# Weight sums by accumulating DMAs, token sums on VectorE, bias rows and decays on ScalarE: one change to a trunk of attention layers and feed-forward blocks

## The chip, the core and the metric

The kernel runs on one core of a Trainium2 chip. The metric is the device time of one execution, in microseconds (us); the median of several runs is given. The engines are TensorE (PE, matmuls; PEld is its weight load), VectorE (DVE), ScalarE (ACT), GpSimd (POOL) and SyncE (SP, which here only issues DMAs). Each engine works through its own list in order and stops at a wait until a semaphore has reached a value. Transfers issued by SP and by GpSimd run in two queues (q1 and q0) on the same 16 DMA engines.

## The reference, cut to what matters

```python
x = x + 0.5 * swiglu(rms_norm(x, g), w_in, w_out)    # FFN, four times
def swiglu(h, w_in, w_out):
    a, b = jnp.split(h @ w_in, 2, axis=-1)           # w_in: 1024 x 5632, w_out: 2816 x 1024
    return (jax.nn.silu(a) * b) @ w_out
# FFN0, sparse attention (NSA), FFN1, shared keys and values, FFN2, forgetting attention (FoX), FFN3
# FoX: softmax(q k^T * scale + c[query] - c[key], causal) v,   c = cumsum(log_sigmoid(f))
# NSA: scores get a bias by bucket of the distance, one column of rel_bias per head
```

There are 256 tokens of 1024 values, in float32.

## The kernel before, in words

**Products.** Each float32 operand is split into a high part (rounded to the matmul's type) and a low part (the rest). A product is three matmuls: high by high, high by low, low by high (`three`, L571 to L573).

**Units.** All weights pass through TensorE in units of 128x2048 values (1.05 MB). For unit u ScalarE casts the high part (`hi(u)`, L1154, `whi`), VectorE subtracts to get the low part (`lo(u)`, L1586, `wlo`), and TensorE multiplies. `whi` and `wlo` are rings of three, so `hi(u)` waits until TensorE is done with unit u-3. Plain units are loaded by SP into a ring of three `raw` buffers (`load`, L448); a load waits until the low part of the buffer's last unit is done. SP works through all of its loads and waits in one order.

**An FFN.** Its hidden columns lie in 11 chunks of 256. The order of the 39 units is `a0 b0 a1 b1 o0 a2 b2 o1 | M1 M5 o2 M2 M6 M3 M7 M4 | a5 b5 o3 a6 b6 o4 | M1 M5 o5 M2 M6 o6 M3 M7 M4 | a9 b9 o7 a10 b10 o8 o9 o10`. `a` and `b` are the two halves of a chunk's input weights (24 matmuls each), `o` its output rows. Chunks 3 and 4, and 7 and 8, are done as pairs: a 2x2 block product with seven products (M1 to M7, 12 matmuls each) in place of eight. For them the four weight blocks B11, B12, B22, B21 of 1.05 MB are loaded by SP (`pair_weights`, L477) into `nat`, `nat`, `work` and `xn`, one after each of four ring loads, from `o0` on for the first pair and from `b5` on for the second. VectorE makes four sums: T1 = B12-B11 (L1674, into `kT` or `low`), T3 = B22-B12 in place (L1681), T2 (L1687) and T4 (L1694). M1, M2, M3 use plain blocks, M5, M7, M6, M4 the sums. The second pair's first load waits for the first pair's sums and for the low part of its M7.

**Token sums.** The pairs need sums of token blocks too. GpSimd joins the high and low parts of the tokens (L2187, twice), multiplies them by the norm's factors (L2193, twice) and makes four sums (L2198 to L2204); ScalarE and VectorE split them (L1231, L1666) before the first pair.

**Hidden.** After a chunk's `b`, ScalarE makes silu(a) (L1215), VectorE multiplies by b (L1644, `gg`), TensorE transposes the result after the `o` units that stand between (L706, into `tb`), ScalarE and VectorE split it (L1221, L1651). In the list of ScalarE for chunk 5 the cast of `a6` stands ahead of silu, that of `b6` behind it; the same holds in the other chunks for the unit three after `a` and the one after that.

**GpSimd's other work.** In FFN0 it builds NSA's bias rows with 32 small copies (L2223), stores them (L2230) and loads them back per head (L2235). In the stage of the shared keys it loads FoX's c for all heads (L2262), and near the end of FFN2 it adds masks and c by query to them, 16 instructions (L2273 to L2277).

Of the kernel before, what the change touches and what calls it, by code (L numbers as in the profile page):

```python
# [27 lines left out]
P = 128  # L28
# [22 lines left out]
RING = 3  # L51
KINDS = "nnnsnnsnn"
# [74 lines left out]
def ring_loads():  # L127

    count, last, loads = [0] * RING, [None] * RING, {}
    for u in range(U_END):  # L130
        if not any(b <= u < b + FFN_UNITS and ORDER[u - b][0] not in "abo" for b in U_FFN):
# [39 lines left out]
def yoco_trunk(nc, x, norm_g, ffn_w_in, ffn_w_out, nsa_w_in, nsa_cmp_pos, nsa_cmp_w1, nsa_cmp_w2,  # L171
               nsa_w_out, rel_bias, kv_norm_g, fox_w_kvf, fox_b_f, fox_w_q, fox_w_out, final_g, out):
    ctx = ExitStack()
    with ctx:
# [87 lines left out]
        b11, b12, b21, b22 = nat[:, 0:UNIT], nat[:, UNIT:2 * UNIT], xn[:, :, :].rearrange("p t n -> p (t n)"), work[:, 0:UNIT]  # L262
# [24 lines left out]
        def combined(f):  # L287

            return low[:, :] if f == 2 else kT[:, :, :].rearrange("p k n -> p (k n)")

# [12 lines left out]
        def unit_source(u):  # L303

            if u in LOADS:
                return raw[LOADS[u][0]][:, :]
            f, b, (kind, j) = of_ffn(u)
            x = combined(f)
            return {"M1": b11, "M2": b21, "M3": b22, "M5": x, "M6": b11, "M7": b12, "M4": x}[kind]
# [31 lines left out]
        s_rows = sem("bias_rows")  # L341
        s_rows_out = sem("bias_rows_stored")
# [10 lines left out]
        s_b11 = sem("b11_loaded")  # L353
        s_b12 = sem("b12_loaded")
# [73 lines left out]
        s_cq = sem("c_by_query")  # L428
        s_decay = sem("decay_ready")
# [17 lines left out]
        def _(sp):  # L447
# [29 lines left out]
            def pair_weights(f, n, i):  # L477
# [21 lines left out]
            def ffn(f):  # L499
                b, n, i = U_FFN[f], 0, None  # L500
                for u, (kind, j) in enumerate(ORDER, b):
# [12 lines left out]
                    if i is not None and kind in "abo":  # L514
# [624 lines left out]
        def _(act):  # L1139
            def hi(u):  # L1140
# [5 lines left out]
                elif kind in ("M1", "M2", "M3"):  # L1146
                    arrived = {"M1": s_b11, "M2": s_b21, "M3": s_b22}[kind]
                    act.wait_ge(arrived, 32 * (len(PAIRS) * f + PAIRS.index(j) + 1))
                else:
                    done = ["M5", "M7", "M6", "M4"].index(kind) + 1  # L1150
                    act.wait_ge(s_tw, 4 * (len(PAIRS) * f + PAIRS.index(j)) + done)
# [81 lines left out]
            def ffn_chunk(f, j, rows):  # L1233
# [13 lines left out]
                hi(a + 3)  # L1247
                act.wait_ge(s_g, 2 * (NSEG * f + i))
# [4 lines left out]
                for r in rows:  # L1253
                    u = b + UNIT_OF["o", r]
                    chunk_hidden_hi(f, j)
                    if u + 3 < b + FFN_UNITS:
                        hi(u + 3)

# [313 lines left out]
        def _(dve):  # L1572
# [95 lines left out]
            def t1_weights(f, j):  # L1668

                n = len(PAIRS) * f + PAIRS.index(j) + 1  # L1670
                dve.wait_ge(s_b11, 32 * n)
                dve.wait_ge(s_b12, 32 * n)
                dve.wait_ge(s_alo, 4 * f + 4)
                dve.tensor_tensor(combined(f), b12, b11, ALU.subtract).then_inc(s_tw, 1)  # L1674

            def t3_weights(f, j):

                n = len(PAIRS) * f + PAIRS.index(j) + 1
                dve.wait_ge(s_b22, 32 * n)
                dve.wait_ge(s_tw, 4 * n - 3)  # L1680
                dve.tensor_tensor(b12, b22, b12, ALU.subtract).then_inc(s_tw, 1)  # L1681

            def t2_weights(f, j):

                n = len(PAIRS) * f + PAIRS.index(j) + 1
                dve.wait_ge(s_tw, 4 * n - 2)
                dve.tensor_tensor(b11, b12, b11, ALU.add).then_inc(s_tw, 1)  # L1687

            def t4_weights(f, j):
# [3 lines left out]
                dve.wait_ge(s_tw, 4 * n - 1)  # L1693
                dve.tensor_tensor(combined(f), b21, b11, ALU.subtract).then_inc(s_tw, 1)  # L1694

            def ffn_chunk(f, j, rows):
# [12 lines left out]
                if pair:  # L1709
                    t1_weights(f, pair)  # L1710
# [4 lines left out]
                if pair:  # L1715
                    t3_weights(f, pair)
# [9 lines left out]
            def ffn_pair(f, j, rows):  # L1726
# [4 lines left out]
                lo(m["M1"] + 3)  # L1731
                t4_weights(f, j)
                lo(m["M5"] + 3)
# [11 lines left out]
                dve.tensor_tensor(c12, tb[1][:, :], c12, ALU.add).then_inc(s_c12, 1)  # L1745
# [8 lines left out]
                dve.tensor_tensor(c22, c22, u3, ALU.add).then_inc(s_c22, 1)  # L1754
# [359 lines left out]
            dve.wait_ge(s_decay, H // 4)  # L2114
# [34 lines left out]
        def _(pool):  # L2149
# [29 lines left out]
            def token_sums(f):  # L2179
# [9 lines left out]
                pool.wait_ge(s_whole, 2 * f + 2)  # L2189
                pool.wait_ge(s_rc, f + 1)  # L2190
                for t in range(NT):
                    tok = slice(t * P, (t + 1) * P)
                    pool.tensor_tensor(m[:, :, tok], m[:, :, tok],  # L2193
                                       rstd_row[:, tok].unsqueeze(1).broadcast_to([P, KT, P]),
                                       ALU.mult).then_inc(s_an, 1)
                pool.wait_ge(s_an, 2 * f + 2)
                a11, a12, a21, a22 = [quarter(m, a) for a in ("A11", "A12", "A21", "A22")]
                pool.tensor_tensor(four(c22), a21, a22, ALU.add).then_inc(s_as, 1)  # L2198
                pool.wait_ge(s_as, 4 * f + 1)
                pool.tensor_tensor(a21, a11, a21, ALU.subtract).then_inc(s_as, 1)  # L2200
                pool.wait_ge(s_as, 4 * f + 2)
                pool.tensor_tensor(a11, four(c22), a11, ALU.subtract).then_inc(s_as, 1)
                pool.wait_ge(s_as, 4 * f + 3)
                pool.tensor_tensor(a12, a12, a11, ALU.subtract).then_inc(s_as, 1)  # L2204

            token_sums(0)
# [6 lines left out]
            pool.wait_ge(s_used, 8)  # L2213
# [3 lines left out]
            after = UNIT_OF["a", PAIRS[0] + 2]  # L2217
            pool.wait_ge(s_setup, 2)
            pool.wait_ge(s_used, after + 1)
            starts = bucket_starts()  # L2220
            for b in range(NB):
                near, far = starts[b], starts[b + 1] - 1
                pool.tensor_copy(rows[:, SEQ - 1 - far:SEQ - near],  # L2223
                                 tbT[:, b:b + 1].broadcast_to([H, far - near + 1]))
            pool.memset(rows[:, SEQ:2 * SEQ], NEG).then_inc(s_rows, 1)
            pool.wait_ge(s_rows, 1)

            pool.dma_start(scratch_b.rearrange("c h m -> h c m"),  # L2230
                           rows.unsqueeze(1).broadcast_to([H, 16, 512])).then_inc(s_rows_out, 16)
            pool.wait_ge(s_rows_out, 16)
            for h in range(H):
                pool.wait_ge(s_used, after + 4 + h)
# [23 lines left out]
            token_sums(1)  # L2258
# [6 lines left out]

            pool.wait_ge(s_cb, 16)
            pool.wait_ge(s_cq, 1)
            token_sums(2)
# [33 lines left out]
```

## Time and profile before

| | |
|---|---|
| time, median of 3 runs | 1044.06 us (1043.92 to 1044.14) |
| profiled execution | 1042.84 us, its span 1041.1 us |
| TensorE busy | 1028.7 us (99%), granted clock 0.997 |
| VectorE, ScalarE, GpSimd busy | 765.6, 587.4, 151.6 us |
| DMA | 182.78 MB, mean 176 GB/s |

A profile shows one execution. In rows of the trace the first numbers are the start and the length in us; "x2" means that two instructions follow one another; brackets at the end give the idle time of the engine before the instruction and what ended it. The busy share of an engine tells how full it is over the whole span; whether a unit came late is seen from TensorE's waits.

### The profile page before, as it was taken

The page shows a single profiled execution, that of the slowest core. Times are in us where ns is not written, and L with a number is a line of the kernel's source. Part 1 is how long each engine was busy: PE and PEld are TensorE (multiplying, and loading weights), DVE is VectorE, ACT ScalarE, POOL GpSimd, SP SyncE. Part 2 cuts the span into 40 slices and gives each one's busy share as a digit, 9 for nine tenths or more (in the row PEclk, how much of TensorE's full clock was granted, in tenths as well). Part 3 has the DMA queues.
Part 4 walks back from the last instruction along what each step waited for, and adds up shares of the span by engine and source line. Part 5 has one row for each costly group of instructions (what it writes and reads, how often), then busy time and mean ns, then how long its engine had stood idle before and what let it go on. Part 6 is the DMA issues. An engine that isn't in the chain of part 4 may idle for free.

```text
span 1041.1 us, 13003 instructions
## 1 busy us (share of the span) xinstructions
PE 1028.7 (99%) x5076; PEld 847.2 (81%) x5076; DVE 765.6 (74%) x925; ACT 587.4 (56%) x732; POOL 151.6 (15%) x140
## 2 busy tenths in 40 slices
PE   8999999999999999999999999999999999999997
PEld 7888888888888888788888888788888888878886
DVE  6897875677576579868656769868766657986864
ACT  6565454656476565555456555546446656555543
POOL 3613111000013150000000150000470015000000
PEclk9999999999999999999999999999999999999999
DMA  9919456457401492742746692752646149274261
GB/s 307 340 23 375 151 155 224 144 181 216 148 2 41 123 341 61 273 171 82 228 145 194 220 345 83 252 193 81 206 158 202 42 141 341 64 269 175 82 202 41
DMA packets 112349, 182.78 MB, mean 176 GB/s; under 512 B 5960, under 2 KB 67504, under 8 KB 112160
## 3 DMA queue, kind: packets, MB, share of 16 engines
q1 hardware_dynamic: 110656, 176.18, 50.2%
q0 software_dynamic: 1456, 5.72, 1.9%
q8 instruction: 40, 0.66, 0.3%
q14 instruction: 21, 0.17, 0.0%
q10 hardware_dynamic: 176, 0.05, 0.0%
HBM read 180.34 MB, written 1.59 MB: 175 GB/s over the span
## 4 chain that ended last, share of the span: by engine, by line
PE 92%; DVE 4%; issue 2%; ACT 1%; DMA 0%; ACTq 0%; DVEq 0%
PE acc L571 13%; PE acc L573 13%; PE acc L572 13%; PE inb L571 12%; PE inb L573 12%; PE inb L572 12%; PE acc L837 2%; PE inb L864 2%; PE tb L849 2%; PE tb L572 1%; PE tb L573 1%; PE tb L571 1%; PE tb L706 1%; DVE wlo L1586 1%; PE inb L861 1%
## 5 line engine op out<-in xcount | busy, mean ns | idle before, releaser
L1586 DVE TENSOR_TENSOR wlo<-raw,whi 128x2048 fp32r<-128x2048 f32 x131 | 319.8, 2443 | 107.9 <-ACT whi L1154 107.7
L1154 ACT CAST whi<-raw 128x2048 fp32r<-128x2048 f32 x131 | 250.5, 1915 | 52.3 <-PE inb L573 19.9
L571 PE MATMUL inb<-whi,thi 128*128 128x512 f32 x528 | 210.1, 398 | 0.6 <-DVE work L1751 0.6
L573 PE MATMUL inb<-whi,tlo 128*128 128x512 f32 x528 | 206.2, 391 | 0.0
L572 PE MATMUL inb<-wlo,thi 128*128 128x512 f32 x528 | 205.9, 390 | 0.0
L571 PE MATMUL acc<-whi,fhi 128*128 128x512 f32 (+1 forms) x384 | 149.0, 388 | 0.0
L573 PE MATMUL acc<-whi,flo 128*128 128x512 f32 (+1 forms) x384 | 148.3, 386 | 0.0
L572 PE MATMUL acc<-wlo,fhi 128*128 128x512 f32 (+1 forms) x384 | 148.2, 386 | 0.0
L571 PEld LDWEIGHTS inb<-whi,thi 128*128 128x128 f32 x528 | 99.3, 188 | 21.4 <-issue 2.2
L573 PEld LDWEIGHTS inb<-whi,tlo 128*128 128x128 f32 x528 | 99.2, 188 | 21.2
L572 PEld LDWEIGHTS inb<-wlo,thi 128*128 128x128 f32 x528 | 99.4, 188 | 19.4
L571 PE MATMUL acc<-whi,thi 128*128 128x512 f32 x224 | 89.5, 399 | 0.8 <-DVE tlo L1614 0.6
L573 PE MATMUL acc<-whi,tlo 128*128 128x512 f32 x224 | 87.6, 391 | 0.0
L572 PE MATMUL acc<-wlo,thi 128*128 128x512 f32 x224 | 87.4, 390 | 0.0
L573 PEld LDWEIGHTS acc<-whi,flo 128*128 128x128 f32 (+1 forms) x384 | 70.5, 184 | 15.9
L572 PEld LDWEIGHTS acc<-wlo,fhi 128*128 128x128 f32 (+1 forms) x384 | 70.5, 184 | 15.4
L571 PEld LDWEIGHTS acc<-whi,fhi 128*128 128x128 f32 (+1 forms) x384 | 70.5, 184 | 15.3
L1215 ACT ACTIVATE sa<-inb,rstd 128x256 f32<-128x256 f32 x48 | 20.2, 470 | 75.6 <-PE inb L573 75.6
L1221 ACT CAST fhi<-tb 128x512 fp32r<-128x512 f32 x28 | 16.4, 587 | 81.6 <-PE tb L706 81.6
L1154 ACT CAST whi<-nat 128x2048 fp32r<-128x2048 f32 x24 | 45.9, 1914 | 22.5 <-PE inb L573 15.4
L1586 DVE TENSOR_TENSOR wlo<-nat,whi 128x2048 fp32r<-128x2048 f32 x24 | 54.9, 2287 | 3.0 <-ACT whi L1154 2.8
L571 PEld LDWEIGHTS acc<-whi,thi 128*128 128x128 f32 x224 | 42.1, 188 | 10.8 <-DVE tlo L1614 1.0
(293 smaller groups left out, 1534.3 us busy)
## 6 DMA issues: line engine op xcount, KB each, us to landing
raw<-in_ffn_w_in SPq DMA_DIRECT2D x110, 512.0 KB, 5.2
raw<-in_ffn_w_out SPq DMA_DIRECT2D x88, 512.0 KB, 5.4
nat<-in_ffn_w_in SPq DMA_DIRECT2D x32, 512.0 KB, 6.4
raw<-in_nsa_w_in SPq DMA_DIRECT2D x20, 512.0 KB, 4.2
work<-in_ffn_w_in SPq DMA_DIRECT2D x16, 512.0 KB, 8.2
xn<-in_ffn_w_in SPq DMA_DIRECT2D x16, 512.0 KB, 10.4
raw<-in_fox_w_kvf SPq DMA_DIRECT2D x16, 512.0 KB, 4.3
raw<-in_nsa_cmp_w SPq DMA_DIRECT2D x8, 512.0 KB, 5.0
```

The costliest lines, as they stand in the source:

```text
L571: pe.matmul(o, lh, rh, start=start, stop=False, skip_group_check=True)
L572: pe.matmul(o, lh, rl, start=False, stop=False, skip_group_check=True)
L573: return pe.matmul(o, ll, rh, start=False, stop=stop, skip_group_check=True)
L706: mm = pe.transpose(tb[0][:, k * SEQ + t * P:k * SEQ + (t + 1) * P], gg[:, t, k * P:(k + 1) * P], ident[:, :])
L837: mm = pe.matmul(acc[2 * (n % 2) + h][:, c0:c0 + keys], qT[rows, p, t * P:(t + 1) * P], kT[rows, kidx, 0:keys], start=True, stop=True)
L849: mm = pe.transpose(tb[h][:, i * P:(i + 1) * P], probs[:, n % 2, c:c + P], ident[:, :])
L861: mm = pe.matmul(o0, pT[:, n % 2, h, 0:P], v(0), start=True, stop=True)
L864: mm = pe.matmul(o1, pT[:, n % 2, h, (1 + k) * P:(2 + k) * P], v(k), start=k == 0, stop=k == 1)
L1154: act.copy(whi[u % RING][:, :], unit_source(u)).then_inc(s_hi, 1)
L1215: act.activation(sa[:, t, :], banks[t][:, 0:FC], ACT.Silu, scale=rstd[:, t:t + 1]).then_inc(s_silu, 1)
L1221: act.copy(hidden_hi[:, k:k + 2, :].rearrange("p k n -> p (k n)"), tb[0][:, :]).then_inc(s_ghi, 1)
L1586: dve.tensor_tensor(wlo[u % RING][:, :], unit_source(u), whi[u % RING][:, :].bitcast(F32), ALU.subtract).then_inc(s_lo, 1)
```

## The change

- B11 is loaded twice: raw through the ring, where M1 is a plain unit now (`PLAIN`), and into `sum_a`. B22 is loaded twice too, into `sum_b` and into `work`. B12 is not loaded alone.
- GpSimd issues two accumulating DMAs per pair (`add_blocks`): `sum_a` += B12 when `sum_a` has landed, `sum_b` += B12 when `sum_b` has. These are T1 and T3, with other signs, and ScalarE casts them when the DMAs have landed.
- VectorE keeps two sums per pair, `sum_a` += B22 (T2) and `sum_a` += B21 (T4); T4 stands behind the low part of M6 instead of M2's. Two later adds become subtractions.
- The second pair's first load waits for the low part of M4 in place of M7.
- The token multiplies and sums move from GpSimd to VectorE, into chunk 1 behind the split of chunk 0's hidden values; GpSimd keeps the join.
- NSA's bias rows are copied by ScalarE in chunks 1 and 2 of FFN0, and their store and the small loads move accordingly; the loads per head wait for later units.
- FoX's masks are added by two accumulating DMAs (into `bias` and into `decay0`, which is loaded by itself), and c by query by ScalarE in chunks 1, 2, 5 and 9 of FFN2.

```diff
+PLAIN = ("a", "b", "o", "M1")
...
                 elif i == 0:
-                    u = b + UNIT_OF["M7", PAIRS[n - 1]]
-                    sp.wait_ge(s_tw, 4 * (len(PAIRS) * f + n))
+                    u = b + UNIT_OF["M4", PAIRS[n - 1]]
+                    sp.wait_ge(s_tw, 2 * (len(PAIRS) * f + n))
                     sp.wait_ge(s_lo, u + 1)
                 if i == 0:
-                    pair_in(f, j, 0, 0, b11, s_b11)
+                    pair_in(f, j, 0, 0, sum_a, s_la)
                 elif i == 1:
-                    pair_in(f, j, 0, 1, b12, s_b12)
+                    pair_in(f, j, 1, 1, sum_b, s_lb)
...
+                    elif kind == "M1":
+                        r = raw[LOADS[u][0]][:, :].rearrange("p (k n) -> p k n", k=4)
+                        w = ffn_w_in[f // 2, f % 2][0:512, j * FC:j * FC + CW].rearrange("(k p) n -> p k n", p=P)
+                        load(u, [(r[:, k:k + 2], w[:, k:k + 2]) for k in (0, 2)])
...
+                    n = len(PAIRS) * f + PAIRS.index(j) + 1
+                    ready = {"M2": (s_b21, 32 * n), "M3": (s_b22, 32 * n), "M5": (s_t1, 16 * n), "M7": (s_t3, 16 * n),
+                             "M6": (s_tw, 2 * n - 1), "M4": (s_tw, 2 * n)}
+                    act.wait_ge(*ready[kind])
...
+            def decays(j, i):
+
+                where = {1: 1, 2: 1, PAIRS[0] + 2: 0, PAIRS[1] + 2: 0}
...
+                act.wait_ge(s_mask1 if t else s_mask0, 16)
+                for h in range(4 * half, 4 * half + 4):
+                    d = bias[:, h, :] if t else decay0[:, h, :]
+                    ins = act.activation(d, d, ACT.Identity, bias=cq[:, t, h:h + 1])
+                ins.then_inc(s_decay, 1)
...
-            def t1_weights(f, j):
...
-                dve.tensor_tensor(combined(f), b12, b11, ALU.subtract).then_inc(s_tw, 1)
...
-            def t3_weights(f, j):
+            def token_sums(f):
...
+                m = whole_tokens(f)
+                dve.wait_ge(s_whole, 2 * f + 2)
+                dve.wait_ge(s_rc, f + 1)
...
                 elif before == 0:
                     chunk_hidden_lo(f, 0)
+                    token_sums(f)
...
                 lo(m["M1"] + 3)
+                lo(m["M5"] + 3)
                 t4_weights(f, j)
-                lo(m["M5"] + 3)
                 lo(m["M5"] + 4)
...
+            def add_blocks(f, n):
+
+                j, m = PAIRS[n], len(PAIRS) * f + n + 1
+                w = ffn_w_in[f // 2, f % 2][0:512, j * FC + DFF:j * FC + DFF + CW].rearrange("(k p) n -> p k n", p=P)
+                for to, begun, added in ((sum_a, s_la, s_t1), (sum_b, s_lb, s_t3)):
+                    pool.wait_ge(begun, 32 * m)
+                    pool.dma_start(to.rearrange("p (k n) -> p k n", k=4), w, accum_op=ALU.add).then_inc(added, 16)
```

## Rows read from the trace of the kernel before

**Rows 1.** The page: busy time of each engine.

```profile
PE 1028.7 (99%) x5076; PEld 847.2 (81%) x5076; DVE 765.6 (74%) x925; ACT 587.4 (56%) x732; POOL 151.6 (15%) x140
```

**Rows 2.** TensorE's waits: line, waited for, us in total, times, longest.

```profile
PE acc L917 <- POOL ident L2160: 1.6, 1, 1.6
...
PE inb L571 <- DVE work L1751: 0.6, 4, 0.2
```

**Rows 3.** Groups by line, VectorE: busy us, mean ns, idle before.

```profile
L1681 DVE TENSOR_TENSOR nat<-work,nat 128x2048 f32<-128x2048 f32 x8 | 18.3, 2283 | 0.0
```

**Rows 4.** Groups by line, GpSimd, then VectorE.

```profile
L2193 POOL TENSOR_TENSOR kT<-kT,work 128x1024 f32<-128x1024 f32 x6 | 21.9, 3667 | 25.4 <-ACT work L1243 25.4
...
L1754 DVE TENSOR_TENSOR work<-work 128x512 f32<-128x512 f32 x8 | 5.5, 692 | 0.3
...
L2140 DVE TENSOR_TENSOR xn<-xs,vx 128x1024 f32<-128x1024 f32 x2 | 2.5, 1225 | 0.1
```

**Rows 5.** Stretches: busy us of each engine, clock, DMA share, GB/s.

```profile
425.00:452.00 27.00, 26.84 (x124) 21.66 (x123) 20.30 (x18) 12.58 (x11) 0.00 (x0) 1.00 1.02 372
...
25.00:50.00 25.00, 25.00 (x117) 20.65 (x117) 19.85 (x18) 14.22 (x16) 17.17 (x6) 1.00 1.00 352
```

**Rows 6.** In order of time, VectorE (M7's and M4's low parts), then SP.

```profile
419.74 2.29 DVE L1586 TENSOR_TENSOR wlo<-nat,whi 128x2048 fp32r<-128x2048 f32 x1 [0.62 <-ACT whi L1154]
...
422.55 2.28 DVE L1586 TENSOR_TENSOR wlo<-kT,whi 128x2048 fp32r<-128x2048 f32 x1
...
422.11 0.88 SPq L475 DMA_DIRECT2D nat<-in_ffn_w_in  x2
```

**Rows 7.** In order of time: FFN1's second pair, ScalarE and VectorE; then FFN3's.

```profile
442.32 1.91 ACT L1154 CAST whi<-raw 128x2048 fp32r<-128x2048 f32 x1 [0.58 <-DMA raw<-in_ffn_w_in]
...
452.41 1.92 ACT L1154 CAST whi<-nat 128x2048 fp32r<-128x2048 f32 x1 [2.92 <-PE inb L573]
...
458.58 1.91 ACT L1154 CAST whi<-kT 128x2048 fp32r<-128x2048 f32 x1
...
444.26 2.29 DVE L1586 TENSOR_TENSOR wlo<-raw,whi 128x2048 fp32r<-128x2048 f32 x1 [1.91 <-ACT whi L1154]
...
939.26 2.29 DVE L1586 TENSOR_TENSOR wlo<-raw,whi 128x2048 fp32r<-128x2048 f32 x1 [2.15 <-ACT whi L1154]
...
947.16 1.91 ACT L1154 CAST whi<-nat 128x2048 fp32r<-128x2048 f32 x1 [2.67 <-PE inb L573]
```

**Rows 8.** FFN1 before its first pair: ScalarE, VectorE, SP, landings from 372 us.

```profile
386.45 0.59 ACT L1221 CAST fhi<-tb 128x512 fp32r<-128x512 f32 x1 [3.35 <-PE tb L706]
386.93 1.92 ACT L1154 CAST whi<-raw 128x2048 fp32r<-128x2048 f32 x1
...
397.42 0.84 ACT L1215 ACTIVATE sa<-inb,rstd 128x256 f32<-128x256 f32 x2 [3.53 <-PE inb L573]
...
377.17 2.88 DVE L1586 TENSOR_TENSOR wlo<-raw,whi 128x2048 fp32r<-128x2048 f32 x1 [1.18 <-ACT whi L1154]
...
376.27 1.25 SPq L475 DMA_DIRECT2D xn<-in_ffn_w_in  x2
...
xn<-in_ffn_w_in SPq DMA_DIRECT2D x2, 512.0 KB, 10.4
```

**Rows 9.** DMA at 585:597 us (two), 349:361, 98:107 (two), whole (one).

```profile
q0 software_dynamic: 144, 2.10, 45.0%
...
raw<-in_ffn_w_in SPq DMA_DIRECT2D x2, 512.0 KB, 9.5
...
raw<-in_ffn_w_in SPq DMA_DIRECT2D x2, 512.0 KB, 4.3
...
q0 software_dynamic: 144, 0.52, 29.8%
...
bias_rows_dram<-low POOLq DMA_DIRECT2D x1, 512.0 KB, 7.8
...
bias<-bias_rows_dram POOLq DMA_DIRECT2D x16, 128.0 KB, 3.2
```

More of the change, by code:

```diff
@@ L130, in ring_loads @@
     for u in range(U_END):
-        if not any(b <= u < b + FFN_UNITS and ORDER[u - b][0] not in "abo" for b in U_FFN):
+        if not any(b <= u < b + FFN_UNITS and ORDER[u - b][0] not in PLAIN for b in U_FFN):
             slot = len(loads) % RING
@@ L307, in unit_source @@
             f, b, (kind, j) = of_ffn(u)
-            x = combined(f)
-            return {"M1": b11, "M2": b21, "M3": b22, "M5": x, "M6": b11, "M7": b12, "M4": x}[kind]
+            return {"M2": b21, "M3": b22, "M5": sum_a, "M6": sum_a, "M7": sum_b, "M4": sum_a}[kind]
         onat = xn[:, :, :].rearrange("p t (h d) -> p t h d", h=H)
@@ L341, in yoco_trunk @@
         s_rows = sem("bias_rows")
+        s_fill = sem("bias_rows_filled")
         s_rows_out = sem("bias_rows_stored")
@@ L1247, in ffn_chunk @@
                 hi(a + 3)
+                if f == 2:
+                    decays(j, 0)
+                elif f == 0:
+                    bias_rows(j, 0)
                 act.wait_ge(s_g, 2 * (NSEG * f + i))
@@ L1257, in ffn_chunk, with bias_rows @@
                         hi(u + 3)
+                if f == 2:
+                    decays(j, 1)
+                elif f == 0:
+                    bias_rows(j, 1)
+            def bias_rows(j, i):
+                if j not in (1, 2):
+                    return
+                act.wait_ge(s_setup, 2)
+                starts = bucket_starts()
+                half = 2 * (j - 1) + i
+                for b in range(NB // 4 * half, NB // 4 * (half + 1)):
+                    near, far = starts[b], starts[b + 1] - 1
+                    ins = act.copy(rows[:, SEQ - 1 - far:SEQ - near], tbT[:, b:b + 1].broadcast_to([H, far - near + 1]))
+                ins.then_inc(s_rows, 1)
+            def decays(j, i):
+                where = {1: 1, 2: 1, PAIRS[0] + 2: 0, PAIRS[1] + 2: 0}
+                if j not in where:
+                    return
+                t, half = where[j], 2 * (j in (2, PAIRS[1] + 2)) + i
+                act.wait_ge(s_cq, 1)
+                act.wait_ge(s_mask1 if t else s_mask0, 16)
[3 more added lines that the diff above has]
+                ins.then_inc(s_decay, 1)
             def ffn_pair(f, j, rows):
@@ L1692, in t4_weights @@
                 dve.wait_ge(s_b21, 32 * n)
-                dve.wait_ge(s_tw, 4 * n - 1)
-                dve.tensor_tensor(combined(f), b21, b11, ALU.subtract).then_inc(s_tw, 1)
+                dve.tensor_tensor(sum_a, sum_a, b21, ALU.add).then_inc(s_tw, 1)
             def ffn_chunk(f, j, rows):
@@ L2188, in token_sums @@
                                        ALU.add).then_inc(s_whole, 1)
[L2189 to L2206, printed above, removed]
+            def add_blocks(f, n):
[4 more added lines that the diff above has]
+                    pool.dma_start(to.rearrange("p (k n) -> p k n", k=4), w, accum_op=ALU.add).then_inc(added, 16)
+            pool.memset(rows[:, SEQ:2 * SEQ], NEG).then_inc(s_fill, 1)
+            join_tokens(0)
+            add_blocks(0, 0)
+            pool.wait_ge(s_rows, 4)
+            pool.wait_ge(s_fill, 1)
+            pool.dma_start(scratch_b.rearrange("c h m -> h c m"),
+                           rows.unsqueeze(1).broadcast_to([H, 16, 512])).then_inc(s_rows_out, 16)
             small = [(gate_w[:, :, :], nsa_w_in[0, :, D + 6 * KVD:].rearrange("(k p) n -> p k n", p=P)),
@@ L2212, in _ @@
                      (bf[:, :], fox_b_f.rearrange("(h a) -> h a", a=1))]
-            pool.wait_ge(s_used, 8)
             for dst, src in small:
                 pool.dma_start(dst, src).then_inc(s_small2, 16)
[L2217 to L2231, printed above, removed]
+            for n in range(1, len(PAIRS)):
+                add_blocks(0, n)
             pool.wait_ge(s_rows_out, 16)
             for h in range(H):
-                pool.wait_ge(s_used, after + 4 + h)
+                pool.wait_ge(s_used, min(UNIT_OF["M4", PAIRS[-1]] + 1 + h // 2, FFN_UNITS))
                 pool.dma_start(bias[:, h, :], bass.AP(tensor=scratch_b.tensor, offset=h * 512 + P - 1,
@@ L2257, in _ @@
             pool.memset(vx[:, :].rearrange("p (i n) -> p i n", n=VP)[:, :, DH], 1.0).then_inc(s_ones, 1)
-            token_sums(1)
+            join_tokens(1)
+            for n in range(len(PAIRS)):
+                add_blocks(1, n)
             pool.wait_ge(s_neg, 1)
```

84 lines of the change are left out of this document (43 added, 41 removed).

## The prediction, made before the result was known

> **What bounds the kernel now.** I read the table of engines first: TensorE is busy 1028.7 us of a span of 1041.1 [rows 1]. The list of TensorE's waits comes next: its largest entry is 1.6 us, once, at the start, and the largest that belongs to the weight pairs is 0.6 us in four pieces, the wait for VectorE's add of `u3` [rows 2]. So TensorE goes from one weight unit to the next without a gap. The change removes no matmul. Whatever it frees on VectorE, GpSimd or ScalarE is worth nothing unless a TensorE wait ends earlier, and it costs nothing until a unit arrives late. The question is therefore how much room each unit has, and the smallest room is where it must be asked: in the stretches in which the DMA engines are full. The table of stretches shows one, behind the first load of FFN1's second pair: 372 GB/s and a DMA share of 1.02 from 425 to 452 us [rows 5]. A share of 1.02 is no spare at all. At 372 GB/s one block of 1.05 MB takes 2.8 us.
>
> **Part by part.**
>
> *Two weight sums fewer on VectorE.* Per pair T1 and T3 go, operations of one shape, 2.28 us each [rows 3]: 16 x 2.28 = 36.5 us of VectorE. TensorE hardly waits for it, so the gain is bounded by [rows 2], 0.6 us. I take 0: that wait (`u3` after the low part of `a5`) hangs on the cast of `a5`, not on a sum. T2 and T4 stay, T4 one unit later, still before its user.
>
> *Token sums to VectorE.* The two GpSimd multiplies took 3.67 us each [rows 4]. They become VectorE's, with the four sums. VectorE does a 128x1024 operation in 1.23 us and a 128x512 one in 0.69 [rows 4], so two and four make 2 x 1.23 + 4 x 0.69 = 5.2 us, once per FFN, right after the hidden split of chunk 0. Behind them wait the low part of `a2` and the gated tiles of chunk 1. In FFN1 VectorE was free from 377.17 - 1.18 = 376.0, and the low part of `a2` ran 377.2 to 380.1 [rows 8]. It would end at 376.0 + 5.2 + 2.3 = 383.5, the tiles at 384.4; the next hidden transposes start 386.4, as ScalarE's cast behind them at 386.45 shows [rows 8]. Cost 0, with some 2 us to spare; FFN0 starts with its loads still arriving; I allow 0.3 us there. From both sides: 0 to 0.3.
>
> *Bias rows and decays to ScalarE.* Eight decay calls of four activations; two of 256 columns take 0.84 us [rows 8], so up to 1.7 us a call, and the bias copies come in four calls of eight short ones. They lie where ScalarE idles 3.3 to 3.5 us per chunk for TensorE [rows 8]. Cost 0. GpSimd's mask additions go; no TensorE wait names them. GpSimd itself now stands at waits for landed blocks; behind them in its list are the masks' transfers, the small loads and the next token join, whose users come a stage later. Both edits, and the sums that leave GpSimd, are costed at nothing beside TensorE's matmuls.
>
> *M1 through the ring, and SP's queue.* The first half B11 is now loaded twice, once raw. SP's load for the second pair waits for the low part of M4 in place of M7. VectorE ended M7's at 419.74 + 2.29 = 422.0 and M4's at 422.55 + 2.28 = 424.8, and SP issued at 422.11 [rows 6]. So the whole burst starts 2.8 us later: behind that wait on SP stand `o3`, `a6`, `b6` and `o4`. The burst has no idle share in which to catch up.
>
> *The accumulating DMAs.* Two blocks of 1.05 MB per pair, on GpSimd's queue. The first starts when the block `sum_a` has landed (about 430 us in FFN1's second pair, plus some 2.5 us, the most of the 3.2 that a 128 KB transfer of this queue takes [rows 9]), the second when `sum_b` has (about 437, so 440). Both fall into the full burst, ahead of the landing of `b6`. Their price is not in this trace. The two nearest rows are GpSimd's plain transfers: 2.10 MB took 45.0% of 12 us = 5.4 us, 2.6 us per MB; 0.52 MB took 29.8% of 9 us = 2.7 us, 5.2 per MB [rows 9]. They do push SP's loads aside: next to the 2.10 MB the `in_ffn_w_in` loads took 9.5 us to land, against 4.3 in the same place of FFN1 [rows 9]. I take 2.8 us per block, the rate of the burst, as these are HBM reads in 2 KB pieces like the pair's own loads; 5.4 is the dear end. Zero is the cheap end, if the engines serve SP's queue first; the 9.5 us speaks against it.
>
> *What is late, then.* In the burst ScalarE waits for landings: its cast of `b6` starts at 442.32 after a wait for the DMA, and VectorE's low part ends 444.26 + 2.29 = 446.55. TensorE needs it when `a6` is done, 452.4, when ScalarE's next cast is released [rows 7]. Room: 5.8 us. In FFN3 the same: 939.26 + 2.29 = 941.55 against 947.1, 5.5 us [rows 7]. The pattern stands four times; I take the mean of the first and last shown, 5.6. Shift of `b6`: 2.8 (later start) + 2 x 2.8 (accumulates) = 8.4 us. Stall: 8.4 - 5.6 = 2.8 us per second pair, four times 11.2. Most of it shows one step earlier, at the transposes before `a6`, because ScalarE casts `a6` before it makes the gated tiles. The duplicate M1 comes behind `o4` and delays only units with more room.
>
> *First pairs.* Their loads are spread by the ring. In FFN1 `o1` is cast at 386.93, so it has landed by then. TensorE needs it when `b2` ends, 397.4 (silu starts there), so its cast must start by 397.4 - 1.9 - 2.3 = 393.2 [rows 8]. With 2.8 us for the first accumulate and some 2 of the second it lands by 391.7. The raw M1 waits for the low part of `a2` (383.5) and then lands behind the pair's last block, which is issued by 377.5 and takes 10.4 [rows 8]: 387.9 + 5.6 + 2.8 = 396.3. TensorE wants M1 after `o1`, 24 matmuls or some 5.4 us behind 397.4, so its cast must start by 398.6. Cost 0, with 1.5 to 2.3 us to spare; FFN0, whose DMA share is 1.00 from 25 to 50 us [rows 5], may have less; I keep 0 for it and leave the rest to the range.
>
> **Sum.** Profiled execution 1042.84 us (span 1041.1 and 1.7 around it). 0 + 0 + 0 + 11.2 + 0 = 11.2, so 1054.0; the median of the three runs lies 1.2 above the profiled one: **1055.3 us**.
>
> **Rivals.**
>
> 1. *Dear accumulates.* At 5.4 us per block `b6` shifts by 2.8 + 10.8 = 13.6, a stall of 8.0 per second pair, 32. First pairs no longer fit: `o1` lands near 395.5 (5.4 for the first, half as fast from the second's start on), low part 399.7 against 397.4, 2.3 us, and about 1 more for the gated tiles behind M1's late cast: 3.3 in three FFNs, and 5 allowed in FFN0. Sum 47: **1091 us**. For it: an accumulate must fetch its destination too, and a row of 5.2 us per MB exists. Against: that row writes to HBM, out of 16 partitions. The Trainium skill (Collectives: The Full Stack, section The bandwidth ceiling: the fold count and why AG ≠ RS ≠ AR) says that an adding DMA gives two read descriptors per chunk on one ring and so runs at about half the rate of a copy. By that rule this rival would be the outcome; no run here shows it yet.
>
> 2. *It fits after all* (not slower). If the engines hold back GpSimd's queue, `b6` shifts by 2.8 alone, against room of 5.6. The point from which it decides: less than 2.8 of the accumulates' 5.6 us ahead of `b6`. Then every cost is hidden: **1044.1 us**. For it: the sums themselves have much time (in FFN1's second pair M5 is cast at 458.58 [rows 7], some 26 us after the first accumulate starts). Against: [rows 9].
>
> 3. *Faster.* VectorE and GpSimd relief removes the 0.6 us of [rows 2] and small delays between units: at most 2 us, **1042 us**. More than that is not in TensorE's list of waits.
>
> 4. *The sum itself comes late.* If an accumulate needs over 26 us, ScalarE stands at M5's cast with TensorE behind it. Ten us more in each of eight pairs would be 80: **1135 us**. Only rates below 40 GB/s do this; the slowest transfer of this queue had 512 KB in 7.8 us, 67 GB/s [rows 9].
>
> **How the numbers follow.** Forecast 0.40, dear accumulates 0.31, fits 0.20, faster 0.04, late sums 0.05. The range takes in the forecast, the dear rival with some us more for the first pairs, and most of the case that fits: 1043.6 to 1096. About 0.2% (2 us) is what a measurement of this kernel can tell from no change. Faster 0.04; same 0.20; slower 0.76.
>
> **What would show it.** Right: TensorE waits for `wlo` of L1586 and for `gg` in four places, some 22 us after each second pair's loads begin; SP's pair load issued 2.8 us after its old place relative to M7; DMA share near 1 for 8 us longer; GpSimd's queue with 16 blocks of 1.05 MB, its share of 16 engines telling 2.8 or 5.4 us each. VectorE 16 us less busy (-36.5, +4 x 5.2). No wait at the first pairs. Wrong: no TensorE wait above 1 us there (rival 2), or waits at `o1` and M1 too (rival 1), or ScalarE waiting for an accumulate's landing (rival 4).

## The result, and the profile after

The changed kernel takes **1107.85 us** (median of 4 runs, 1102.15 to 1111.26), the kernel before 1043.99 us in the same comparison: ratio 1.061, 95% interval 1.058 to 1.063. The forecast was 1055.3 us with a range up to 1096.0; the time lies above the range. Slower was foreseen, 11 us of it; it is 64.

The page of the changed kernel: engines, TensorE's granted clock in 40 slices, GpSimd's queue (packets, MB, share of the 16 engines), and landings (median us from issue to landing last).

```profile
span 1109.2 us, 13021 instructions
...
PE 1046.1 (94%) x5076; PEld 858.0 (77%) x5076; DVE 737.3 (66%) x933; ACT 600.0 (54%) x796; POOL 80.2 (7%) x87
...
PEclk9999899999899999989999999989999999998999
...
q0 software_dynamic: 14304, 25.64, 12.1%
...
nat<-in_ffn_w_in POOLq DMA_DIRECT2D x16, 1024.0 KB, 13.9
...
bias<-cmask POOLq DMA_DIRECT2D x1, 1024.0 KB, 18.4
```

Beside [rows 1]: TensorE runs the same 5076 matmuls but is busy 17.4 us longer; VectorE works 28.3 us less and GpSimd 71.4 us less, which buys nothing, since TensorE did not wait for them before. The waits say where the rest is. TensorE's first, then ScalarE's longest (line, waited for, us in total, times, longest):

```profile
PE tb L712 <- DVE gg L1682: 39.7, 6, 9.7
PE inb L577 <- DVE wlo L1624: 5.5, 2, 3.5
PE acc L577 <- DVE wlo L1624: 4.9, 2, 4.7
...
ACT whi L1159 <- DMA raw<-in_ffn_w_in: 105.4, 18, 14.4
```

TensorE's three entries are 50.1 us that [rows 2] did not have. Pauses 50.1 + longer matmuls 17.4 = 67.5 of the 68.1 us by which the span grew. TensorE names VectorE, VectorE waits for ScalarE, and ScalarE stands up to 14.4 us at loads of plain input units: the weight loads come late.

One of the places, FFN1's second pair, in order of time: SP's and GpSimd's issues, then ScalarE, VectorE and TensorE (start, length, idle before in brackets).

```profile
448.76 0.88 SPq L477 DMA_DIRECT2D nat<-in_ffn_w_in  x2
...
452.24 0.94 SPq L457 DMA_DIRECT2D raw<-in_ffn_w_in  x2
...
459.25 11.29 SPq L457 DMA_DIRECT2D raw<-in_ffn_w_in  x2
...
454.07 1.25 POOL L2235 DMA_DIRECT2D nat<-in_ffn_w_in  x1 [51.23 <-DMA nat<-in_ffn_w_in]
460.45 1.29 POOL L2235 DMA_DIRECT2D nat<-in_ffn_w_in  x1 [5.12 <-DMA nat<-in_ffn_w_in]
...
473.72 1.90 ACT L1159 CAST whi<-raw 128x2048 fp32r<-128x2048 f32 x1 [13.77 <-DMA raw<-in_ffn_w_in]
...
479.43 1.90 ACT L1159 CAST whi<-raw 128x2048 fp32r<-128x2048 f32 x1 [3.07 <-DMA raw<-in_ffn_w_in]
...
475.65 2.29 DVE L1624 TENSOR_TENSOR wlo<-raw,whi 128x2048 fp32r<-128x2048 f32 x1 [13.26 <-ACT whi L1159]
477.86 0.87 DVE L1682 SCALAR_TENSOR_TENSOR gg<-inb,rstd,sa 128x256 f32<-128x256 f32 x2
...
478.78 1.12 PE L712 MATMUL tb<-ident,gg 128*128 128x128 f32 x4 [8.54 <-DVE gg L1682]
...
480.13 0.63 PE L578 MATMUL inb<-wlo,thi 128*128 128x512 f32 x1
```

The same in the kernel before: SP's issues of `a6` and `b6`, and ScalarE's cast of `a6`.

```profile
428.39 0.93 SPq L455 DMA_DIRECT2D raw<-in_ffn_w_in  x2
...
431.92 0.97 SPq L455 DMA_DIRECT2D raw<-in_ffn_w_in  x2
...
436.60 1.92 ACT L1154 CAST whi<-raw 128x2048 fp32r<-128x2048 f32 x1 [0.51 <-DMA raw<-in_ffn_w_in]
```

The two ring loads at 452.24 and 459.25 are `a6` and `b6`. `a6` is issued 3.5 us after the pair's first load and lands at 473.7, when its cast can start: 21.5 us in flight, where before it was 8.2. While it was in flight, GpSimd's accumulates were issued, at 454.1 and 460.5. SP itself is held: giving out `b6` took it 11.29 us, where it took 0.97 us before. In the last row of the changed kernel a matmul takes 0.63 us, where the same matmul takes 0.40 at the full clock.

The DMA engines while both accumulates ran, 460 to 474 us (packets, MB, share), and then the stretches around (busy us of PE, PEld, DVE, ACT, POOL; clock, DMA share, GB/s):

```profile
q0 software_dynamic: 991, 1.96, 75.6%
q1 hardware_dynamic: 1150, 1.48, 34.8%
...
449.00:460.00 11.00, 10.82 (x52) 8.58 (x51) 9.13 (x10) 5.41 (x5) 1.25 (x1) 1.00 0.94 324
460.00:474.00 14.00, 10.25 (x45) 8.02 (x43) 2.39 (x2) 0.28 (x1) 1.29 (x1) 0.95 1.10 246
474.00:485.00 11.00, 6.22 (x21) 5.15 (x22) 5.97 (x5) 5.04 (x6) 0.00 (x0) 0.60 1.06 387
```

75.6% of 14 us for 1.96 MB is 5.4 us per MB: twice what the plain transfer of the same queue took in [rows 9]. The engines are full (share 1.10) and move 246 GB/s, against 372 in [rows 5]. Behind the pause the granted clock is 0.60. How the two queues share the engines is seen in 7 us in which both have work, 460 to 467 (packets, MB, share):

```profile
q0 software_dynamic: 541, 1.08, 82.9%
q1 hardware_dynamic: 539, 0.54, 28.4%
```

There is one packet of SP's for each of GpSimd's. But GpSimd's carry 2 KB and take 82.9% x 7 us x 16 engines / 541 = 172 ns each; SP's here carry 1 KB and take 59 ns. So the due loads get less than a third of the engines' time: 0.54 MB in 7 us, 77 GB/s.

### The profile page after: what moved, and what is told of

It is laid out like the page before. It is cut to its first block, busy times and chain, and to the rows that moved or that the text cites. A ratio compares the mean times of both kernels' runs of the same rounds, so it can differ in the third digit from the quotient of the medians.

```text
span 1109.2 us, 13021 instructions
## 1 busy us (share of the span) xinstructions
PE 1046.1 (94%) x5076; PEld 858.0 (77%) x5076; DVE 737.3 (66%) x933; ACT 600.0 (54%) x796; POOL 80.2 (7%) x87
## 4 chain that ended last, share of the span: by engine, by line
PE 69%; DMA 14%; DVE 8%; ACT 4%; issue 3%; SPq 2%; ACTq 0%; DVEq 0%
DMA raw<-in_ffn_w_in 12%; PE acc L577 10%; PE acc L579 10%; PE acc L578 10%; PE inb L577 8%; PE inb L578 8%; PE inb L579 8%; DVE wlo L1624 5%; ACT whi L1159 3%; PE acc L843 2%; PE inb L870 2%; PE tb L855 2%; DMA raw<-in_ffn_w_out 1%; PE tb L579 1%; PE tb L578 1%
## 5 line engine op out<-in xcount | busy, mean ns | idle before, releaser
L1624 DVE TENSOR_TENSOR wlo<-raw,whi 128x2048 fp32r<-128x2048 f32 x139 | 326.5, 2350 | 205.4 <-ACT whi L1159 205.2
L1159 ACT CAST whi<-raw 128x2048 fp32r<-128x2048 f32 x139 | 265.6, 1913 | 186.8 <-DMA raw<-in_ffn_w_in 105.4
L577 PE MATMUL inb<-whi,thi 128*128 128x512 f32 x528 | 215.4, 408 | 6.2 <-DVE wlo L1624 5.5
L578 PE MATMUL inb<-wlo,thi 128*128 128x512 f32 x528 | 210.3, 398 | 0.0
L579 PE MATMUL inb<-whi,tlo 128*128 128x512 f32 x528 | 209.8, 397 | 0.0
L578 PEld LDWEIGHTS inb<-wlo,thi 128*128 128x128 f32 x528 | 102.3, 194 | 20.3
L1624 DVE TENSOR_TENSOR wlo<-nat,whi 128x2048 fp32r<-128x2048 f32 x32 | 73.2, 2288 | 19.4 <-ACT whi L1159 19.4
L1159 ACT CAST whi<-nat 128x2048 fp32r<-128x2048 f32 x32 | 61.1, 1910 | 21.5 <-PE acc L579 14.7
L712 PE MATMUL tb<-ident,gg 128*128 128x128 f32 x112 | 19.5, 302 | 39.7 <-DVE gg L1682 39.7
L712 PEld LDWEIGHTS tb<-ident,gg 128*128 128x128 f32 x112 | 14.9, 154 | 45.5 <-DVE gg L1682 42.6
## 6 DMA issues: line engine op xcount, KB each, us to landing
nat<-in_ffn_w_in POOLq DMA_DIRECT2D x16, 1024.0 KB, 13.9
```

The costliest lines, as they stand in the source:

```text
L577: pe.matmul(o, lh, rh, start=start, stop=False, skip_group_check=True)
L578: pe.matmul(o, lh, rl, start=False, stop=False, skip_group_check=True)
L579: return pe.matmul(o, ll, rh, start=False, stop=stop, skip_group_check=True)
L712: mm = pe.transpose(tb[0][:, k * SEQ + t * P:k * SEQ + (t + 1) * P], gg[:, t, k * P:(k + 1) * P], ident[:, :])
L1159: act.copy(whi[u % RING][:, :], unit_source(u)).then_inc(s_hi, 1)
L1624: dve.tensor_tensor(wlo[u % RING][:, :], unit_source(u), whi[u % RING][:, :].bitcast(F32), ALU.subtract).then_inc(s_lo, 1)
```

## The experiments

Each theory has to say which part of the change costs the 64 us, and whether it is a price, a place or a clock. All ratios are against the kernel before, run on the same chip at the same time.

**1. Without the weight sums' DMAs.**

```diff
-                for to, begun, added in ((sum_a, s_la, s_t1), (sum_b, s_lb, s_t3)):
-                    pool.wait_ge(begun, 32 * m)
-                    pool.dma_start(to.rearrange("p (k n) -> p k n", k=4), w, accum_op=ALU.add).then_inc(added, 16)
+                pool.wait_ge(s_lb, 32 * m)
```

> The changed kernel without its 16 accumulating transfers of 1 MB into the weight blocks (the sums T1 and T3 lack the term B12; the two mask transfers stay). Theory: the 64 us come from these transfers alone; the later start of the second pair's loads (2.8 us), the second copy of B11, the token sums on VectorE and the bias and decay work on ScalarE all lie inside room of over 5 us. Then 1044 to 1047 us, TensorE waits for gg (L1682 or its line) under 1 us in all, TensorE busy near 1029 us. Rival: SP's later wait and the second copy of B11 cost by themselves; then 1050 us or more, with the waits in the same four places.

Measured: 1043.73 us, ratio 1.000 (0.999 to 1.001). The page's engine row and queue row:

```profile
PE 1027.9 (99%) x5076; PEld 846.7 (81%) x5076; DVE 737.7 (71%) x933; ACT 600.1 (58%) x796; POOL 59.4 (6%) x71
...
q0 software_dynamic: 5856, 8.87, 4.2%
```

Everything else of the change (token sums on VectorE, bias rows and decays on ScalarE, M1 through the ring, the later start of the pair's loads, the masks' DMAs) costs nothing together, as long as the 16 accumulates are not there. The later start is real: SP's first pair load moved from 422.11 to 425.03 us. It is hidden, as these rows show (here the cast of `a6`, the gated tiles behind its low part, the transposes; then the transposes of before):

```profile
439.91 1.91 ACT L1159 CAST whi<-raw 128x2048 fp32r<-128x2048 f32 x1 [3.69 <-DMA raw<-in_ffn_w_in]
...
444.06 0.87 DVE L1682 SCALAR_TENSOR_TENSOR gg<-inb,rstd,sa 128x256 f32<-128x256 f32 x2
...
446.36 0.60 PE L712 MATMUL tb<-ident,gg 128*128 128x128 f32 x4
...
446.24 0.60 PE L706 MATMUL tb<-ident,gg 128*128 128x128 f32 x4
```

`a6` lands at 439.91, the tiles are ready 5.0 us later at 444.93, and TensorE takes them at 446.36: 1.4 us of room. Before, it landed at 436.60 and was needed at 446.24, so by the same 5.0 us it had 4.6.

**2. Plain copies in the accumulates' place**: same bytes, same queue, same waits, no addition (B12 overwrites the block).

```diff
-                    pool.dma_start(to.rearrange("p (k n) -> p k n", k=4), w, accum_op=ALU.add).then_inc(added, 16)
+                    pool.dma_start(to.rearrange("p (k n) -> p k n", k=4), w).then_inc(added, 16)
```

> The changed kernel with the 16 transfers as plain copies of the same bytes from the same queue (B12 overwrites the block, the addition is left out). Theory: an accumulating packet of 2 KB costs an engine 176 ns where SP's plain packets of that size cost 84 to 95, and that price decides: plain ones should cost some 90 ns, land in 7 to 9 us in place of 13.5, and the shift of a6 falls from 10.5 us to about 5; 1050 to 1062 us. Rival: GpSimd's queue takes its share of the engines whatever it carries, and SP's loads starve alike: 1090 us or more.

Measured: 1066.15 us, ratio 1.022 (1.019 to 1.025), TensorE busy 1036.9 us. TensorE's waits, the copies' landing, and the q0 share in 14 us (436 to 450) of FFN1's second pair:

```profile
PE tb L712 <- DVE gg L1682: 7.8, 4, 3.5
PE inb L577 <- DVE wlo L1624: 3.0, 2, 1.5
PE acc L577 <- DVE wlo L1624: 2.2, 1, 2.2
...
nat<-in_ffn_w_in POOLq DMA_DIRECT2D x16, 1024.0 KB, 9.3
...
q0 software_dynamic: 544, 2.10, 39.5%
```

39.5% of 14 us for 2.10 MB is 2.6 us per MB. At this price, close to the one the forecast took, the pauses are 13.0 us, against a forecast of 11.2: 10.8 us at the four second pairs, and 2.2 in FFN2's first pair, where the forecast had none. So the argument from room and burst held; the price did not. TensorE is again busy 8.2 us longer, which no term of the forecast had, and the time is 4 us above the band expected. One thing besides the addition differs: the copy goes in 544 packets of 3.9 KB, 163 ns each, not in 2 KB ones.

**3. The same accumulates, issued later**: the first after ScalarE has cast `o1` or `b6`, the second after it has cast M1.

```diff
+                first, second = ((("o", 1), ("M1", j)) if n == 0 else (("b", 6), ("M1", j)))
+                for to, begun, added, unit in ((sum_a, s_la, s_t1, first), (sum_b, s_lb, s_t3, second)):
                     pool.wait_ge(begun, 32 * m)
+                    pool.wait_ge(s_hi, U_FFN[f] + UNIT_OF[unit] + 1)
```

> The changed kernel with all its accumulating transfers, each issued later by a wait on GpSimd: in first pairs after the casts of o1 and of M1, in second pairs after the casts of b6 and of M1, when SP's loads of a6, b6 and o4 have landed. Same work, same price. Theory: what costs is that they stand in the engines beside loads that are due; issued behind them they cost nothing where the sum still comes in time (M5's cast in the second pair must start within some 12 us of b6's cast): 1044 to 1052 us. Rival: the added volume or their price as such costs, wherever they run: over 1070 us.

Measured: 1050.52 us, ratio 1.007 (1.005 to 1.008), TensorE busy 1030.5 us.

```profile
PE tb L577 <- DVE wlo L1624: 2.4, 3, 1.7
...
nat<-in_ffn_w_in POOLq DMA_DIRECT2D x16, 1024.0 KB, 13.7
```

The accumulates take as long as before to land (13.7 against 13.9 us) and 9 tenths of the loss are gone. So the accumulates cost where they stand in the burst; the work of adding costs little elsewhere. What is left stands at M5, which now waits for its sum, above all in FFN2's first pair.

**4. Only the second accumulate late** (the first in its place).

```diff
                 for to, begun, added in ((sum_a, s_la, s_t1), (sum_b, s_lb, s_t3)):
+                    if to is sum_b:
+                        pool.wait_ge(s_hi, U_FFN[f] + UNIT_OF["M1", j] + 1)
```

> The changed kernel with the first accumulate of each pair in its place and only the second delayed until ScalarE has cast M1. Theory: the pauses come from the accumulates standing in front of due loads, each with its 5.4 us, on top of a start that is 2.8 us later. With one of them, a6 and b6 shift by 2.8 + 5.4 = 8.2 us against room of 5.6: some 2.6 us of pause at each second pair, 10.5 us in all, no pause at the first pairs of FFN0 and FFN1, and 5 to 10 us more of TensorE busy time if pauses of that size lower the clock: 1056 to 1066 us. Rival: nearly all harm is done by the second accumulate, since it keeps the engines taken until a6 is due. Then this kernel stands where both late additions stood, near 1051 us. Second rival: the first alone does it, since it comes right in front of a6. Then it stays above 1090 us.

Measured: 1068.73 us, ratio 1.023 (1.021 to 1.025), TensorE busy 1038.4 us.

```profile
PE tb L712 <- DVE gg L1682: 13.4, 5, 3.8
PE inb L577 <- DVE wlo L1624: 1.5, 1, 1.5
```

14.9 us of pauses, and 9.7 of longer matmuls. Neither rival holds: one accumulate does somewhat over a third of the harm, since the first has to use up the room that the later start left before the second costs in full. The time is 3 us above the band expected; the pauses were 2.9 to 3.8 us at the second pairs in place of 2.6, and FFN2's first pair added 1.5. The expectation took the 5.6 us of room of `b6`; `a6` has 1 us less.

**5. to 7. Late loads without any added transfer.** The kernel before, with nothing of the change; only SP's load of `a6` waits. The diff is that of the first, which waits for VectorE's low part of `o3`; the second waits for TensorE's end of `b5` (`s_used`), the third for its end of `o3`.

```diff
                     elif kind in "ab":
+                        if (kind, j) == ("a", 6):
+                            sp.wait_ge(s_lo, b + UNIT_OF[("o", 3)] + 1)
```

> The kernel before, with nothing of the change, but SP's load of a6 waits in every FFN until VectorE has made the low part of o3. In FFN1 of before that is 438.0 us, 2.9 us ahead of the end of b5, for which the earlier kernel (late by b5) waited; its four pauses were 5.2 us each, so here they should be about 2.3 us each, 9 us in all. Theory: a pause of TensorE costs its own length and, behind it, a stretch at the lower clock. If short pauses do that too, TensorE's busy time rises by 5 to 10 us above 1028.7 and the median is 1057 to 1063 us. Rival: only long pauses lower the clock. Then the busy time stays at 1029 and the median is 1052 to 1054 us.

> The kernel before, with SP's load of a6 held back in each FFN until TensorE is done with b5 (a pause of TensorE by itself, with none of the change). By the rows of before: issue at 440.9, landing 446.2, cast to 448.1, low part 450.4, gated tiles 451.3, so TensorE stands 4.9 us before the transposes at 446.4, four times 20 us. Theory: a TensorE pause costs more than itself when the granted clock falls to half afterwards, and short pauses cost only themselves: 1064 us with the clock at full, 1074 or more if it falls after each.

> The same with the load of a6 held back until TensorE is done with o3: issue 446.5, landing 451.8, pause about 10.5 us, four times 42 us. Theory: after such a pause the clock is at its lower level for some 10 us, as in the changed kernel after its 9.7 us pauses, and that costs half of it again, 5 us each: about 1106 us. Rival: the pauses cost only themselves, 1086 us, and the 17 us more of TensorE busy time in the changed kernel have another cause (contention with the transfers).

Measured: 1062.05 us (ratio 1.017, 1.016 to 1.019), 1075.51 (1.030, 1.029 to 1.032) and 1095.58 (1.051, 1.048 to 1.053). Waits, in this order:

```profile
PE tb L708 <- DVE gg L1646: 8.7, 4, 2.2
```

```profile
PE tb L708 <- DVE gg L1646: 20.5, 4, 5.2
```

```profile
PE tb L708 <- DVE gg L1646: 43.4, 4, 11.2
```

The first two lie in the bands expected; the third is 10 us below what was expected and 10 above its rival. TensorE's busy time rose by 7.2, 10.0 and 7.4 us: about 2 us behind each of four pauses, whether the pause was 2.2 us long or 11.2. Stretches of the first of these kernels show it:

```profile
452.00:455.00 3.00, 0.81 (x6) 0.69 (x6) 2.26 (x3) 0.00 (x0) 0.00 (x0) 1.00 1.10 360
455.00:458.00 3.00, 3.00 (x9) 2.33 (x9) 0.85 (x1) 2.38 (x2) 0.00 (x0) 0.57 1.05 397
458.00:468.00 10.00, 10.00 (x43) 8.20 (x43) 7.63 (x5) 4.12 (x4) 0.00 (x0) 0.96 0.86 323
```

TensorE idles 2.2 us in the first line at a granted clock of 1.00; in the 3 us behind it the clock is 0.57, so nearly all of them at the lower level (1.2 GHz in place of 2.4), and it starts 9 matmuls where at 43 in 10 us some 13 would fit. So longer matmuls follow from pauses, without any added transfer, and the rival of that run, that only long pauses lower the clock, falls. In the third kernel the clock is down while TensorE still idles, as 463 to 466 us of it show, so part of the slow time costs nothing there, which is why it came out below its expectation:

```profile
463.00:466.00 3.00, 0.00 (x0) 0.00 (x0) 0.00 (x0) 1.26 (x1) 0.00 (x0) 0.50 1.07 391
```

**8. Without the masks' accumulates**, so without FoX's masks.

```diff
-                act.wait_ge(s_mask1 if t else s_mask0, 16)
+                act.wait_ge(s_cb if t else s_cb0, 16)
...
-            pool.dma_start(bias[:, :, P:SEQ], masks, accum_op=ALU.add).then_inc(s_mask1, 16)
...
-            pool.dma_start(decay0, masks, accum_op=ALU.add).then_inc(s_mask0, 16)
```

> The changed kernel without its two accumulating mask transfers (1 MB each, SBUF to SBUF, FFN2; the causal mask is left out of FoX). The first took 18.4 us just when FFN2's first loads are due, and FFN2's first pair had two pauses at b2 and o1 where FFN1's had one at M1. Theory: FFN2 then looks like FFN1 and 4 to 8 us go, about 1100 us. Rival: the mask transfer only used spare room, since the kernel without weight adds ran at the old time with the masks in it: no change from 1107 us, within 2.

Measured: 1101.53 us, ratio 1.056 (1.055 to 1.057): 5 to 6 us less than the whole change. In FFN2, where the masks are added, TensorE's pauses went from 2.0, 4.7 and 7.2 us to 1.1, 2.5 and 5.1. The profiles alone do not show that this is the masks': between the same two executions the pauses of FFN0 and of FFN1 shrank by 2.5 and 2.3 us too, where no mask is added.

**9. The early start back.** In FFN0, 1 and 3, T4 goes into `kT`, so the second pair's first load can wait for M7 again.

```diff
-            return {"M2": b21, "M3": b22, "M5": sum_a, "M6": sum_a, "M7": sum_b, "M4": sum_a}[kind]
+            last = sum_a if f == 2 else kT[:, :, :].rearrange("p k n -> p (k n)")
+            return {"M2": b21, "M3": b22, "M5": sum_a, "M6": sum_a, "M7": sum_b, "M4": last}[kind]
...
-                    u = b + UNIT_OF["M4", PAIRS[n - 1]]
+                    u = b + UNIT_OF["M4" if f == 2 else "M7", PAIRS[n - 1]]
```

> The changed kernel with T4 written to its own block (kT) in FFN0, 1 and 3, so that SP's loads for the second pair wait for the low part of M7 as before, not for M4's: they start 2.8 us earlier in three FFNs. Theory: in a full burst a later start is paid in full once the room is used up, so the pause before a6 shortens by 2.8 us in each: 8 us less, about 1099 us. Rival: the burst's length is set by the transfers' work, and a6 starves until both adds are done whatever the start: less than 3 us gained.

Measured: 1096.71 us, ratio 1.051 (1.049 to 1.052).

```profile
PE tb L713 <- DVE gg L1683: 26.0, 6, 5.8
```

This is 10 to 11 us less than the whole change, against 3 x 2.8 = 8.4 expected: the 2.8 us that cost nothing in experiment 1 are paid in full once the room is gone.

**10. Silu ahead of the cast of `a6`.** For chunk 5, `silu` and `gg` go before the cast of `a6`, and on VectorE `gg` before its low part.

```diff
-                    hi(a + 3)
+                    if j != 5:
+                        hi(a + 3)
...
+                    if j == 5:
+                        hi(a + 3)
```

> The changed kernel with ScalarE's silu and VectorE's gated tiles of chunk 5 put ahead of the cast and low part of a6. Theory: TensorE's long wait is for gg only because both engines stand at a6 first; with the order turned it waits for a6's low part in place of gg, in the same places and at most 1.5 us shorter each: 1101 to 1107 us, the entry for gg (L712 or its line) gone from TensorE's waits and the one for wlo longer by as much. Rival: the wait for gg has a cause of its own; then most of the 40 us go with it.

Measured: 1102.19 us, ratio 1.057 (1.056 to 1.059).

```profile
PE inb L577 <- DVE wlo L1627: 26.7, 8, 6.2
PE tb L712 <- DVE gg L1685: 6.7, 3, 2.9
```

At the second pairs the wait moves from `gg` to the low part of the late unit; the 6.7 us left at `gg` stand at first pairs, which the edit does not touch. That TensorE names `gg` is a matter of ScalarE's order; the late load is what it waits for.

**11. Experiments 3 and 9 together**, and FFN2's first accumulate already behind `b2`'s cast (the diff is against experiment 3).

```diff
-                first, second = ((("o", 1), ("M1", j)) if n == 0 else (("b", 6), ("M1", j)))
+                first, second = ((("b", 2) if f == 2 else ("o", 1), ("M1", j)) if n == 0 else (("b", 6), ("M1", j)))
```

> The kernel with late adds (1050.5 us) with the early start of the run before in FFN0, 1 and 3, and FFN2's first add issued after the cast of b2 in place of o1. The late adds left pauses at M5, since the first add landed 466.65 where M5's cast had to start by 465. Theory: with the loads 2.8 us earlier the add lands in time in three second pairs, and FFN2's first pair by its earlier issue: 1044 to 1047 us, no better than the kernel before, since TensorE is full. Rival: the remaining 7 us are the price of 2 MB more per pair in the engines anyhow: 1050 us again.

Measured: 1047.28 us, ratio 1.0035 (1.0022 to 1.0047), TensorE busy 1028.5 us, one wait for a weight unit left.

```profile
PE tb L713 <- DVE gg L1683: 2.3, 1, 2.3
```

The whole change, placed elsewhere, costs 3.7 us. It is no faster than before, as TensorE was full there and the change takes no matmul away. The one pause ends at 641.07, and the 10 us behind it limit what experiments 5 to 7 say of the clock:

```profile
641.00:651.00 10.00, 9.93 (x44) 7.85 (x45) 8.97 (x6) 9.39 (x11) 0.00 (x0) 1.00 1.05 248
```

The granted clock is 1.00 throughout, and TensorE is busy no longer than before. So a pause of 2.3 us can also pass without the lower clock. The same holds for the pause of 2.0 us in the changed kernel (at 663.95, FFN2) and one of 2.9 in experiment 4 (at 103.55, FFN0). What decides between these and the four pauses of experiment 5, of 2.1 to 2.3 us, no run shows.

## Why the prediction was wrong

**VectorE's 16 sums, token sums, bias rows and decays: right.** All at nothing, and experiment 1 shows nothing for them together. VectorE is 28.3 us less busy, more than the 16 in the list of signs: the low parts of ring units also take 2350 ns in place of 2443.

**SP's later start: right in size** (2.9 us in experiment 1) and right that the room hides it when it is alone.

**The price of an accumulate: the step that failed.** "I take 2.8 us per block, the rate of the burst." The trace shows 5.4 us per MB, 5.7 per block: the dear end. The forecast chose by likeness to the pair's own loads, HBM reads in 2 KB pieces, and put the 5.2 us row aside for its direction and its 16 partitions. Experiment 2 moves the same bytes without the addition at 2.6 us per MB, but in 3.9 KB packets. What 2 KB packets cost without an addition is seen in SP's queue before, 425 to 452 us:

```profile
q1 hardware_dynamic: 5208, 10.01, 101.2%
```

These carry 1.9 KB and take 101.2% x 27 us x 16 engines / 5208 = 84 ns each, 2.7 us per MB, where an accumulating packet of 2 KB takes 171 (991 of them in the 14 us from 460). So it is the addition that doubles the price, and not the size of the pieces. The Trainium skill (Collectives: The Full Stack, section The bandwidth ceiling: the fold count and why AG ≠ RS ≠ AR) gives an adding DMA about half the rate of a copy; the trace agrees, 5.4 against 2.6 us per MB, though here it is a local load and no collective.

**Room and stall: right in method, with the wrong unit's room.** Rival 1 put the dear price through the same sum. It has 13.6 us of shift for `b6` and 8.0 us per second pair; the traces have `b6` landing 30.7 us behind the pair's first issue in place of 20.2, with the later start 13.3 in all, and a pause of 8.5 in FFN1. It has 47 us of pauses in all, measured were 50.1. It was right also that the transposes are where it is seen. Two details differ. `a6` was hit as hard as `b6` (it landed 13.3 us later against the old start), because its packets took turns with the accumulates' dearer ones while it was in flight; the sum had delayed only `b6`. And `a6` has the smaller room, 4.6 us (experiment 1) in place of 5.6: 13.3 - 4.6 = 8.7, and the pause measured is 8.5. The masks' DMAs were costed at nothing too; beside the accumulates the kernel takes 5 to 6 us more with them (experiment 8), alone nothing (experiment 1).

**First pairs at 0: wrong for the same reason.** At the dear price the 1.5 to 2.3 us to spare are gone in every FFN: 16 of the 50 us of pauses stand there, in FFN0 at `b2` (3.5 us), in FFN2 at `b2` and `o1` (2.0 and 4.7), in FFN1 and FFN3 at the transposes behind M1's late cast (2.8 each). Rival 1 has 15 for them, and that this comes so near is partly luck: it has 5 us in FFN0 and 3.3 in each of the others.

**The clock: a term that was missing.** Every case was made of pauses only. TensorE pauses nine times more than before for over 0.9 us, and the clock falls at eight of them; 17.4 us of longer matmuls are about 2 us for each, as in experiments 5 to 7. With these 17 us rival 1 would have read 1091 + 17 = 1108 us, and with 2 us for each of its four pauses the forecast 1055 + 8 = 1063, near the 1066 of the plain copies. The trace of before had no pause above 1.6 us in which this could be seen. It is also why the range missed: its upper end was the dear rival's 1091 with 5 us more, so that with the right price alone the time would have been inside.

**The other rivals.** The sums themselves were in time: an accumulate lands in 13.9 us, well under the 26 at which rival 4 decides, and all late units of the changed kernel are plain ones. Only when they are issued later (experiment 3) does M5 wait. Nothing was faster.

That the extra pauses come from the transfers' share of the engines is shown by experiments 1 to 4. SP's issue of `b6` was held 11.29 us; in experiments 1 and 3, with no transfer of GpSimd's beside it, it took 3.2 us, with the plain copies 5.3. Whether the held issue adds to the delay is not shown: no run tells it apart from the transfers themselves.

## What to carry to other kernels

Ask of every added transfer where in the burst it stands, and price it in engine time, not in bytes: an accumulating DMA took twice that of a copy, and starting it after the due loads gave back nine tenths of the loss. Room is used up by all delays together, so what costs nothing alone (2.8 us of later start) is paid in full beside another. Behind a pause of a full TensorE allow some 2 us more for the lower clock; pauses of 2.0 to 2.9 us came here with it and without.

## What was not expected of the hardware

- Accumulating into SBUF from HBM took 5.4 us per MB of the 16 engines' time against 2.6 for the same bytes as a copy, and 13.9 us to land against 9.3. It went in 2 KB packets of 171 ns, the copy in 3.9 KB packets of 163 ns.
- The two queues took turns packet by packet (541 to 539), so the queue with the dearer packets got 83% of the engines against 28%. By the Trainium skill (DMA: Bandwidth & Descriptors, section Queues, rings and completion order) an engine goes round its queues one packet at a time; the count agrees. With the plain copies it is less even: 186 to 404 from 441 to 444 us of experiment 2, where GpSimd's packets are of 3.9 KB.
- SP's issue of one unit took 11.29 us against 0.97. SP works in order, so what stands behind it in its list is issued later.
- Pauses of 2.2 us were followed by some 3 us at the lower level of TensorE's clock (experiment 5), and pauses of 11 us cost no more behind them (experiment 7); yet behind one of 2.3 us the clock stayed at 1.00 (experiment 11).
